# A hybrid decoder layer: the RWKV inputs of the first 64 tokens are prepared apart from those of the other 192

## The reference

```python
h = rmsnorm(x, norm_mix) * (1 + sc1) + sh1          # sc, sh, gt: six 2048-wide parts of silu(c) @ w_ada
p = h @ w_in                                        # GLA columns | RWKV columns
# GLA heads: chunked gated linear attention -> o_gla
xs = rwkv_p + (prev - rwkv_p) * rwkv_mu             # token shift; new_shift = rwkv_p[:, -1]
r, wl, k7, v7, al, gl7 = split_cols(xs, RWKV_SPLITS)
decay = exp(-exp(w))
S = S * decay + sa x (kk * a) + v7 x k7             # RWKV-7 recurrence over the tokens, 16 heads of 64
y = S r                                             # sa = S (-kk)
bonus = sum(r * k7 * rwkv_r_k) * v7
x = x + gt1 * (concat([o_gla, o_rwkv]) @ w_out)
x = x + gt2 * hier_moe(rmsnorm(x, norm_ffn) * (1 + sc2) + sh2)    # 32 experts, all weights streamed
y = rmsnorm(x, norm_final) * (1 + sc_f) + sh_f      # sh_f, sc_f from silu(c) @ w_ada_final
```

## Time and profile before

| | us |
|---|---|
| median of 3 executions | 1842.2 |
| the three | 1833.71, 1842.2, 1843.66 |
| profiled execution, its time | 1842.56 |
| profiled execution, its span | 1840.5 |
| TensorE busy | 1730.5 (94%) |
| VectorE busy | 704.1 (38%) |
| ScalarE busy | 481.2 (26%) |
| GpSimd busy | 207.8 (11%) |

### The profile page before, as it was taken

The page is one execution under the profiler, slowest core; times in us unless marked ns, Lnnn a source line. Parts: engine busy times, 40 slices in busy tenths (PEclk is TensorE's granted clock), DMA queues, the critical chain, the costliest instruction groups (busy, mean ns, idle before and its releaser), DMA issues.

```text
span 1840.5 us, 36936 instructions
## 1 busy us (share of the span) xinstructions
PE 1730.5 (94%) x16064; PEld 1231.0 (67%) x16064; DVE 704.1 (38%) x1498; ACT 481.2 (26%) x875; POOL 207.8 (11%) x297
## 2 busy tenths in 40 slices
...
DMA packets 118007, 629.76 MB, mean 342 GB/s; under 512 B 9412, under 2 KB 77436, under 8 KB 86399
## 3 DMA queue, kind: packets, MB, share of 16 engines
...
...
## 4 chain that ended last, share of the span: by engine, by line
PE 45%; DMA 12%; DVE 0%; issue 0%; ACT 0%; SPq 0%; DVEq 0%; ACTq 0%
PE pb L3023 19%; DMA ring<-in_w_exp_up 11%; PE pb L3038 6%; PE pb L3002 6%; PE pb L3012 2%; PE pb L3013 2%; PE pb L2344 2%; PE pb L2345 2%; PE pb L2346 2%; DMA ring<-in_w_exp_down 1%; PE pb L3077 1%; PE pb L3046 0%; PE pb L3265 0%; PE pb L3055 0%; PE pb L3052 0%; PE pb L3053 0%
## 5 line engine op out<-in xcount | busy, mean ns | idle before, releaser
L3023 PE MATMUL pb<-ring,pj 128*64 128x256 f32 x4064 | 462.0, 381 | 23.4 <-DMA ring<-in_w_exp_up 23.4
L3023 PEld LDWEIGHTS pb<-ring,pj 128*64 128x64 f32 x4064 | 284.0, 137 | 187.1 <-DMA ring<-in_w_exp_up 35.2
L2344 PE MATMUL pb<-ht_parts,ring_parts 128*128 128x264 f32 x1056 | 308.5, 292 | 6.7 <-DVE ring_parts L1494 6.2
L2345 PE MATMUL pb<-ring_parts 128*128 128x264 f32 x1056 | 301.2, 285 | 0.0
L2346 PE MATMUL pb<-ring_parts 128*128 128x264 f32 x1056 | 300.9, 285 | 0.0
L2344 PEld LDWEIGHTS pb<-ht_parts,ring_parts 128*128 128x128 f32 x1056 | 200.9, 190 | 23.8 <-issue 16.0
L3038 PE MATMUL pb<-ring,pj 128*64 128x512 f32 x960 | 211.9, 594 | 0.0
L2345 PEld LDWEIGHTS pb<-ring_parts 128*128 128x128 f32 x1056 | 201.1, 190 | 0.0
L2346 PEld LDWEIGHTS pb<-ring_parts 128*128 128x128 f32 x1056 | 200.0, 189 | 0.0
L2118 DVE TENSOR_TENSOR pj_parts<-pb,pj_parts 64x512 fp32r<-64x512 f32 x120 | 82.6, 688 | 284.3 <-ACT pj_parts L1332 282.4
L1494 DVE TENSOR_TENSOR ring_parts<-ring,ring_parts 128x2048 fp32r<-128x2048 f32 x50 | 114.6, 2292 | 173.9 <-ACT ring_parts L894 173.8
(11 more groups left out here) (502 smaller groups left out, 1939.8 us busy)
## 6 DMA issues: line engine op xcount, KB each, us to landing
...
```

What stands on the lines that cost most here:

```text
L2344: pe.matmul(out, hi[:, k, :], ht_lo[:, k, :], start=(k == 0), stop=False)
L2345: pe.matmul(out, lo[:, k, :], ht_hi[:, k, :], start=False, stop=False)
L3023: last = pe.matmul(pb[bank][SLOT * h:SLOT * h + SLOT, e * 256:(e + 1) * 256], xg[:, k, SLOT * e:SLOT * e + SLOT], w[:, k, h * 256:(h + 1) ...
```

## The change

Five things are changed.

1. The chunk inputs become a function `chunk_inputs(js, g, done)` of tiles `js` and tokens `g`. Ahead of the loop it is called once, for all eight tiles and the first 64 tokens. For the other 192 tokens it is called twice inside chunk 0, for tiles 0 to 3 after the additions of l = 1 and for tiles 4 to 7 after those of l = 2. The grams of chunk 0 wait for `ck_in` of 2; the `whole` of the sample tokens waits for 4, and the later chunks' grams for 6. The sample tokens' r*k*r_k becomes two operations of its own ahead of the first call, and the clearing of `st` stands there too, behind a wait for `sv_store`.
2. exp(-b) goes to `growth`, a stretch of `ht` that the last projection tile still reads, so ScalarE makes it after its copy of `o_gla`. `sv_row` moves into `s3`.
3. On TensorE piece 1 moves behind the transposes of `sv`, and pieces 2 and 3 into chunk 0, where pieces 4 and 5 get new places after `turned(2)` and `inverse_grow(2)`.
4. ScalarE gathers `sv` after the fourth group of shift rows instead of after the seventh.
5. The low part of `o_gla` (L1837 before) is taken after the additions of l = 3 instead of ahead of l = 1.

```diff
@@ -194,7 +194,8 @@
         rr, rk, rv = pj[:, TR:TR + 8, :], pj[:, TK7:TK7 + 8, :], pj[:, TV7:TV7 + 8, :]
         sv = misc[:, 0:384].rearrange("p (t v b) -> p t v b", v=6, b=NS)
         svt = misc[:, 384:768].rearrange("p (v d) -> p v d", d=RD)
-        sv_row = ht_flat[0:48, 2112:3136]
+        sv_row = s3[0:48, 0:1024]
+        growth = tiles8(ht_flat[:, W8:2 * W8])
         wc = misc[:, 768:800].rearrange("p (t c) -> p t c", c=NCH)
         y8 = ht[:, 8:16, :]
 
@@ -1096,19 +1097,19 @@
             beside(49)
             act.activation(sv[:, :, 1, :], t0[:, :, NP_:NT], ACT.Exp, scale=-HALF_E).then_inc(once("sv_w")[0], 1)
             decay(t0, t1, -HALF_E).then_inc(S("cw_exp"), 1)
-            act.wait_ge(S("cw_exp"), 2)
-            decay(t1, t1, HALF_E).then_inc(S("cw_exp"), 1)
             evac(49)
             act.copy(ht[:, 0:8, :], o_gla).then_inc(once("gla_moved")[0], 1)
             act.wait_ge(S("ev_a"), GLA_TILES // 2 + 26)
+            decay(growth, t1, HALF_E).then_inc(S("cw_exp"), 1)
             for b in range(7):
                 act.wait_ge(S("so_ps"), b + 1)
                 n = min(BANK, RCOLS - b * BANK)
                 act.copy(shift_out[:, b * BANK:b * BANK + n], pb[b % 2][0:COND, 0:n]).then_inc(S("so_evac"), 1)
-            act.wait_ge(*once("kk_done"))
-            for v, src in ((0, rr), (2, rk), (3, rv), (4, ra), (5, rb)):
-                last = act.copy(sv[:, :, v, :], src[:, :, NP_:NT])
-            last.then_inc(once("sv_rest")[0], 1)
+                if b == 3:
+                    act.wait_ge(*once("kk_done"))
+                    for v, src in ((0, rr), (2, rk), (3, rv), (4, ra), (5, rb)):
+                        last = act.copy(sv[:, :, v, :], src[:, :, NP_:NT])
+                    last.then_inc(once("sv_rest")[0], 1)
             act.wait_ge(*once("sv_ps"))
             for b in range(2):
                 last = act.copy(sv_row[:, b * BANK:(b + 1) * BANK], pb[b][0:48, :])
@@ -1738,22 +1739,25 @@
             def pr(x):
                 return x[:, :, 0:NP_]
 
-            dve.wait_ge(S("cw_exp"), 3)
-            for hf in range(2):
-                js = slice(4 * hf, 4 * hf + 4)
-                link(dve.scalar_tensor_tensor(out=ra[:, js, 0:NP_], in0=ra[:, js, 0:NP_], scalar=-1.0, in1=t2[:, js, 0:NP_],
+            def chunk_inputs(js, g, done):
+
+                link(dve.scalar_tensor_tensor(out=ra[:, js, g], in0=ra[:, js, g], scalar=-1.0, in1=t2[:, js, g],
                                               op0=ALU.mult, op1=ALU.mult))
-                for t in range(4 * hf, 4 * hf + 4):
-                    last = dve.scalar_tensor_tensor(out=t2[:, t, :], in0=rr[:, t, :], scalar=vecs[:, V_RK + t:V_RK + t + 1],
-                                                    in1=rk[:, t, :], op0=ALU.mult, op1=ALU.mult)
+                for t in range(js.start, js.stop):
+                    last = dve.scalar_tensor_tensor(out=t2[:, t, g], in0=rr[:, t, g], scalar=vecs[:, V_RK + t:V_RK + t + 1],
+                                                    in1=rk[:, t, g], op0=ALU.mult, op1=ALU.mult)
                 last.then_inc(S("ck_in"), 1)
-                dve.wait_ge(S("ck_in"), 2 * hf + 1)
-                for x, d in ((rr, t0), (rk, t1), (rb, t1)):
-                    last = dve.tensor_tensor(x[:, js, 0:NP_], x[:, js, 0:NP_], d[:, js, 0:NP_], ALU.mult)
+                dve.wait_ge(S("ck_in"), done + 1)
+                dve.wait_ge(S("cw_exp"), 3)
+                for x, d in ((rr, t0), (rk, growth), (rb, growth)):
+                    last = dve.tensor_tensor(x[:, js, g], x[:, js, g], d[:, js, g], ALU.mult)
                 last.then_inc(S("ck_in"), 1)
+
+            LATER = slice(CH, NP_)
+            dve.wait_ge(S("cw_exp"), 2)
+            chunk_inputs(slice(0, 8), GROUPS[0], 0)
             dve.tensor_copy(wc, pr(t0).rearrange("p t (c n) -> p t c n", n=CH)[:, :, :, CH - 1])
-            dve.wait_ge(S("ck_in"), 4)
-            dve.memset(st, 0.0).then_inc(once("ck_zero")[0], 1)
+            dve.wait_ge(S("ck_in"), 2)
             dve.wait_ge(*once("gla_moved"))
             dve.wait_ge(S("consts"), N_CONSTS + N_MASKS)
 
@@ -1832,10 +1836,6 @@
                 if c == 1:
                     dve.tensor_copy(xt[:, :, NP_:NT], x_kept).then_inc(once("x_back")[0], 1)
                     dve.wait_ge(*once("x_back"))
-                if c == 0:
-                    dve.wait_ge(S("o_hi"), 1)
-                    dve.tensor_tensor(ht_lo[:, 0:8, :], ht[:, 0:8, :], ht_hi[:, 0:8, :].bitcast(F32), ALU.subtract)\
-                        .then_inc(S("out_lo"), 1)
                 for l in range(1, 6):
                     if l == 3:
                         bonus_out(c)
@@ -1864,6 +1864,18 @@
                         now = ttm[:, hf, 0:n]
                         dve.tensor_tensor(now, now, pb[T_BANKS[hf]][:, 0:n * 256].rearrange("p (a j n) -> p a j n", a=n, n=CH),
                                           ALU.add).then_inc(S("iv_tn"), 1)
+                    if l == 1 and c == 0:
+                        dve.wait_ge(S("sv_store"), 16)
+                        dve.memset(st, 0.0).then_inc(once("ck_zero")[0], 1)
+                        link(dve.tensor_tensor(t2[:, :, NP_:NT], rr[:, :, NP_:NT], vec(V_RK, 8, NS), ALU.mult))
+                        dve.tensor_tensor(t2[:, :, NP_:NT], t2[:, :, NP_:NT], rk[:, :, NP_:NT], ALU.mult)
+                        chunk_inputs(slice(0, 4), LATER, 2)
+                    if l == 2 and c == 0:
+                        chunk_inputs(slice(4, 8), LATER, 4)
+                    if l == 3 and c == 0:
+                        dve.wait_ge(S("o_hi"), 1)
+                        dve.tensor_tensor(ht_lo[:, 0:8, :], ht[:, 0:8, :], ht_hi[:, 0:8, :].bitcast(F32), ALU.subtract)\
+                            .then_inc(S("out_lo"), 1)
                 ada(c + 4)
                 if c == 0:
                     dve.wait_ge(S("ada_mod"), 5)
@@ -2618,7 +2630,6 @@
 
 
             ada_piece(4, 0)
-            ada_piece(4, 1)
             pe.wait_ge(S("ev_a"), GLA_TILES // 2 + 26)
             for b in range(7):
                 if b == 1:
@@ -2628,14 +2639,13 @@
                 for j in range(4 if b < 6 else 2):
                     last = pe.transpose(pb[b % 2][0:COND, j * P:(j + 1) * P], so_raw[:, 4 * b + j, :], ident[:])
                 last.then_inc(S("so_ps"), 1)
-            ada_piece(4, 2)
             pe.wait_ge(*once("sv_rest"))
             pe.wait_ge(S("so_evac"), 7)
             for t in range(8):
                 last = pe.transpose(pb[t // 4][0:48, (t % 4) * P:(t % 4 + 1) * P],
                                     sv[:, t].rearrange("p v b -> p (v b)"), ident[:])
             last.then_inc(once("sv_ps")[0], 1)
-            ada_piece(4, 3)
+            ada_piece(4, 1)
             pe.wait_ge(S("ki_evac"), 8)
             pe.wait_ge(*once("sv_evac"))
 
@@ -2737,7 +2747,7 @@
                 if c > 0:
                     pe.wait_ge(S("ck_s"), c * 2)
                     pe.wait_ge(S("ck_yev"), c)
-                pe.wait_ge(S("ck_in"), 4)
+                pe.wait_ge(S("ck_in"), 2 if c == 0 else 6)
                 for hf in range(2):
                     for x, bank in zip((rb, rk), G_BANKS[hf]):
                         for j in HALF[hf]:
@@ -2750,19 +2760,23 @@
                         last = pe.matmul(pb[4][r, j * CH:(j + 1) * CH], ra[r, j, now], rb[r, j, now], start=True, stop=True)
                 last.then_inc(S("ck_g"), 1)
                 turned(0, rv, 5)
-                ada_piece(c + 4, 4)
+                ada_piece(c + 4, 2 if c == 0 else 4)
                 inverse_step(1)
                 turned(1, rb, 6)
                 inverse_grow(1)
-                ada_piece(c + 4, 5)
+                ada_piece(c + 4, 3 if c == 0 else 5)
                 inverse_step(2)
                 pe.wait_ge(S("ck_ve"), c * 3 + 1)
                 turned(2, rk, 5)
+                if c == 0:
+                    ada_piece(4, 4)
                 pe.wait_ge(S("ck_ve"), c * 3 + 2)
                 whole(6, t2, GROUPS[c]).then_inc(S("bonus_ps"), 1)
                 inverse_grow(2)
                 if c == 0:
+                    ada_piece(4, 5)
                     pe.wait_ge(S("bonus_ev"), 1)
+                    pe.wait_ge(S("ck_in"), 4)
                     whole(6, t2, GROUPS[NCH]).then_inc(S("bonus_ps"), 1)
                 ada_piece(c + 4, 6)
                 inverse_step(3)
```

## The result

The changed kernel takes **1846.6 us** (median of 20 executions, 1843.5 to 1854.4). The kernel before, measured beside it, takes 1840.3 (20 executions, 1833.7 to 1845.5). The ratio is 1.0042, with a 95% interval of 1.0031 to 1.0053. That is no change by the 0.5% bound, but a small real loss: 6.3 us by the medians, 7.7 by the ratio. The prediction had +5.2 and 1847.8.

A forecast was written before the change was run, and what follows sets the result against it. The prediction took TensorE's own list to bound the RWKV stage; -8.2 + 3.7 + 4.4 + 5.5 + 0 = +5.4 us, rounded down to +5.2, on 1842.56 gave 1847.8 us, range 1837 to 1857.

The forecast's parts named there:

- Start of the grams: At chunk 0's border: the first gram starts at 534.6 us instead of 542.84, -8.2 us.
- Pieces: Pieces 2 and 3 on TensorE inside chunk 0: 2 x 1.82, +3.7 us, with nothing hiding them.
- First stall: Ahead of chunk 0's first growth: TensorE waits for ScalarE, held by the landing of shift-row stores, +4.4 us.
- Second stall: Ahead of chunk 0's sample-token sums: TensorE waits 6.9 us for VectorE's bonus product; less the old 1.4, +5.5 us.
- bare stall: TensorE's wait for chunk 0's bonus product without GpSimd's effect: VectorE's list 13.9 us against TensorE's 9.4, 4.5 us.
- the stretching by GpSimd: In VectorE's second half of later inputs: eight operations lose 0.3 us each beside GpSimd, 2.4 us, between 0 and 8.0.
- rival A: In VectorE's second half each of eight operations waits 1.0 us for a GpSimd instruction: +12.6, 1855.2 us; chance 0.17.
- Clock: Around chunk 0: one low stretch behind each new stall, as many as remain before, 0 us, between -3 and +2.
- The sum: All terms from the border through chunk 0 together: +5.4 us, rounded down to +5.2.
- At nothing: Costs put at zero, among them the later low part of `o_gla` (2.35 us, covered) and GpSimd's recurrence moving.
- B: In chunk 0 only one of the two stalls occurs: -0.1 or +1.0, 1842.5 to 1843.6 us; chance 0.19.
- C: In chunk 0 no stall, and the clock stays high: -4.5 us or more, 1834.9 to 1838 us; chance 0.10.

The follow-up runs named there:

- run 1: The changed kernel with SyncE's twelve stores of shift rows issued ahead of modulation piece 4's load instead of behind it; 1842.6 us, ratio 1.0013.
- run 8: The changed kernel with ScalarE's cast of the attention output behind the emptying of inverse_step(1) instead of ahead of it; 1844.8 us, ratio 1.0028.
- run 3: The changed kernel with GpSimd's sample recurrence held back until VectorE's last inputs are made; 1845.4 us, ratio 1.0025.
- run 9: The kernel of run 1 with two holds of GpSimd, in chunks 1 and 2; 1834.6 us, ratio 0.9981.
- run 10: The kernel of run 4 with two holds of GpSimd, in chunks 1 and 2; 1827.9 us, ratio 0.9932.
- run 4: The changed kernel with the shift-row stores ahead of piece 4's load and VectorE's second half of later inputs after l = 3's level operation; 1830.0 us, ratio 0.9941.

## Why the prediction was right, and where its sizes were off

- **Start of the grams, -8.2:** measured -8.93. The chain of shift rows, `sv` and piece 1 set it, as worked out.
- **Pieces, +3.7:** right; piece 3 took 2.33 us since its start was at the low clock.
- **First stall, +4.4:** 4.93, by the mechanism given (piece 4's load, stores behind it, copy and cast). ScalarE's wait ended 21.8 us after piece 0; predicted was 21.2. Runs 1 and 8 show each link.
- **Second stall, 6.9:** 9.95, the term with the largest error. The bare stall was put at 4.5 and measured 4.58 (run 3). What was mis-sized in it is **the stretching by GpSimd**: "I take 0.3 each, 2.4". It was 5.4 us. GpSimd was put "2 us sooner" and beside the second half alone; it started 5.7 us sooner, counted from piece 0 (30.7 instead of 36.5), since its states landed 5 us sooner during the first stall, and reached the first half too (+1.8). And the eight operations of the second half lost 5.1 us, 0.63 each on average (two, of 0.94 and 0.96, lost nothing): just under the 0.7 at which rival A was said to decide. VectorE's own waits between its operations, 0.9 us in run 3, covered part of both. The single unstretched row, 0.68, was given too much weight against chunk 1's group.
- **Clock, 0:** +2.4. The prediction put one low stretch at each stall, as many as remained before. These two came (at 544 and 565 us, 6.8 and 10.2 us long), but the late one, at 580 before, did not go: it came at 589. Why it should go had not been said.
- **The sum, +5.4,** was +10.65 at chunk 1, and came out near the truth at the end (+6.3) because of two things that the prediction did not have: 2.2 us came back in chunks 1 and 2, where GpSimd now stood more luckily beside VectorE (TensorE waited 2.2 us for its level operations there, before 5.65), and 2.8 behind chunk 3, within what the versions scatter there (1123 to 1128), with no cause tried. That every microsecond at chunk 1 passes to the end, as the prediction assumed, did not hold: about 5 of 10.65 did not. So the case and both mechanisms were right, but the closeness of the number is luck: two errors of 3 and 2.4 us were covered by another of about 5. The absolute figure was built on the profiled execution's 1842.56, 2.2 us above the median measured later; on that median the same sum gives 1845.5, which is 1.1 too low instead of 1.2 too high.
- **"At nothing":** the low part of `o_gla` took 3.18 us instead of 2.35 and was covered. The statement that GpSimd's recurrence has room held: in runs 9 and 10 its last rounds run at 720 us, and TensorE turns its result at 745.6 and 746.0 without a wait.
- **Rivals:** A had the right mechanism at two thirds of its size. B and C did not happen here, but C's line is what run 4 shows once both stalls are removed: it was put at -4.5 to -7.7 us, or 1834.9 to 1838; at chunk 1 run 4 is 5.9 us ahead of the kernel before, and it came out at 1830.0.
